# First four chunks of the second conditioning half: their own buffers, issued from ScalarE's queue

## The chip, the cores and the metric

The kernel runs on one core of a Trainium2 chip. Times are device microseconds (us) of one execution of the whole program; lower is better. The engines are TensorE (PE, matmuls; PEld, its weight loads), VectorE (DVE), ScalarE (ACT), GpSimd (POOL) and SyncE (SP). DMA transfers are issued from the queues of SP (q1 in the DMA lists), ACT (q10) and POOL (q0).

## What is computed

One block of a diffusion backbone: a conditioning vector c is turned by w_ada (2048 x 12288) into six modulation vectors; the first two are needed at once, the other four only later. The modulated latents (512 tokens) and context tokens (256) go through w_in, whose first 1024 columns (xa) feed a recurrent mixer.

```python
mod = silu_c @ w_ada[l] + b_ada[l]
mod_ctx = silu_cc @ w_ada[l] + b_ada[l]
sh1, sc1, g1, sh2, sc2, g2 = jnp.split(mod[:, None, :], N_ADA, axis=-1)
u_ctx = _modulate(_rms_norm(ctx, norm1_g[l]), sh1c, sc1c)
hc_f, hc_b = _bidir_rglru(u_ctx @ w_in[l][:, :D_LRU], *lru_p, h_zero, h_zero)
u = _modulate(_rms_norm(x, norm1_g[l]), sh1, sc1)
mix, _, _ = _mixer(u, rows, h0_f, h0_b, w_in[l], *lru_p, ...)
x = x + g1 * mix
x = x + g2 * _swiglu(_modulate(_rms_norm(x, norm2_g[l]), sh2, sc2), w_ffn_in[l], w_ffn_out[l])
```

## The kernel before, in words

Everything is written with explicit semaphores, one instruction stream for each engine, executed in the order of the code. All matmuls run in float32r as three products of a high and a low part: ACT copies a landed weight slice into its high part (`hi`, L826), DVE subtracts that from the slice to get the low part (`lo`, L2126), and PE multiplies (L1471 to L1473). This document calls the slices of w_in that go through the four-slot ring `w_raw` units; each is 128 x 1024 floats, 512 KB, and is loaded from SP's queue (L418).

**The first conditioning half** (the two modulation vectors that are needed at once) is read in 32 pieces into `ada_pq`, a ring of four slots of 8 KB per partition in the region `lru` (32 KB per partition). PE multiplies them (L1521) and counts them in `ada_used`. They come in eight ranges; after each, DVE and ACT scale and split two of the 16 feature slices of `u` and the context. Between the pieces PE already works on units 0 to 7 of xa.

**After the last range** SP has stored the transposed latents `x_raw` (4 MB, L450) and has issued units 8 and 9 right behind that store. Units 10 and later are each issued when the unit four places earlier has been used up (`unit_used`). The region `lru` now becomes `pad`, which takes the xa results, padded for a convolution: PE's banks are copied out by ACT (`xa_out`, L889) and by DVE (`xa_out`, L2248; it signals `ctx_free`). The first column half (heads 0 to 3) goes into the first 16 KB per partition, the second half (heads 4 to 7) into the last 16 KB. PE begins unit 8 only when the banks of column half 0 have been copied out by both engines. In DVE's stream that copy stands behind `lo` of unit 8 and `lo` of unit 9, and `lo` of unit 9 needs ACT's `hi` of unit 9, which needs unit 9 landed.

**The second conditioning half** is done without PE. It is read in chunks of 512 KB (128 rows of 1024 floats); DVE scales each chunk by one element of silu(c) and adds it to an accumulator (L2133 for the first of 16, L2136 for the others; it counts them in `ada2_used`), and PE sums each accumulator over the partitions at the end (`part_sums`, L1569). The first 32 chunks (0 to 31) are issued from POOL's queue (L755) into `ada2_pa`, four slots in the region `yx` that `x_raw` had; so POOL waits for the store of `x_raw` (`x_stored`) and for the last scaling. Chunk n from 4 on waits until chunk n-4 has been used. DVE takes them in fixed portions between the low parts of the units: behind `lo` of unit 10 chunks 0 to 4, behind `lo` of unit 11 chunks 5 to 9, and so on (`EARLY_CHUNKS`), chunks 28 to 31 behind `lo` of unit 16. PE runs units 8 to 15, then waits for chunk 31 (`part_sums`), then goes on with the windows of the recurrent mixer.

Of the kernel before, what the change touches and what calls it, by code (L numbers as in the profile page):

```python
# [21 lines left out]
F32 = mybir.dt.float32  # L22
# [6 lines left out]
D = 2048  # L29
T = 512  # L30
TC = 256
# [10 lines left out]
PADX = TC + 5  # L42
# [16 lines left out]
EARLY_CHUNKS = {8: 5, 9: 5, 10: 5, 11: 5, 12: 4, 13: 4, 14: 4, 15: 0}  # L59
N_EARLY = 32  # L60
N_MID = N_EARLY + 16
LANDED = (20 * 16, 20 * 16, 12 * 16, 12 * 16)


NPAIR = D_FF // P
# [39 lines left out]
class Chain:  # L105
# [5 lines left out]
    def link(self, ins):  # L111
        self.n += 1
        ins.then_inc(self.sem, 1)
        self.eng.wait_ge(self.sem, self.n + self.shift)
# [10 lines left out]
def build(nc, x, c, ctx_in, c_ctx, w_ada, b_ada, norm1_g, norm2_g, w_in, conv_w, conv_b, lru_wa, lru_ba,  # L125
          lru_wx, lru_bx, lru_lambda, w_lru_out, w_pool, pool_scale, w_fourier, b_gate, w_out,
          w_ffn_in, w_ffn_out, norm_f_g, consts, dft, out, x_fm):
    with ExitStack() as stack:

        kb = 1024  # L130
# [10 lines left out]
        def sb(name, region, shape, dt=F32, off=0):  # L141
            return nc.alloc_sbuf_tensor_at(name, [P, *shape], dt, offset=where[region] + off)
# [33 lines left out]
        pad = sb("pad", "lru", [HEADS, 1024])  # L176
# [72 lines left out]
        xcv_l = sb("xcv_l", "ada", [TCAT], F32R, 3 * kb)  # L249
        dft_t = sb("dft_t", "mix", [3, T], F32, 16 * kb)  # L250
        ada2_pa = sb("ada2_pa", "yx", [4, 1024])
        ada2_pc = sb("ada2_pc", "pf", [2, 1024])
        ada2_pw = sb("ada2_pw", "u_hi", [4, 1024], F32, 16 * kb)
        ada2_acc = sb("ada2_acc", "ada", [1024], F32, 8 * kb)
# [11 lines left out]
        cvec = misc("cvec", [KT, 2])  # L266
# [482 lines left out]
        @block.gpsimd  # L749
        def _(pool):  # L750
            def chunk(n, dst, slot=None):

                i, cc = n // 16, n % 16
                slot = n % 4 if slot is None else slot
                pool.dma_start(dst, ada_t[:, cc, 2 * D + 1024 * i:2 * D + 1024 * i + 1024]).then_inc(ada2_landed[slot], 16)  # L755

            pool.wait_ge(x_stored, 16)
            pool.wait_ge(u_aff, 2 * KT)
            for n in range(N_EARLY):
                if n >= 4:  # L760
                    pool.wait_ge(ada2_used, n - 3)
                chunk(n, ada2_pa[:, n % 4, :])
            for n in range(N_EARLY, N_MID):
                pool.wait_ge(ada2_used, n - 1)
                chunk(n, ada2_pc[:, n % 2, :], n % 2)
            for m in range(16):
                slot = (2, 3, 0, 1)[m % 4]
                if m == 2:
                    pool.wait_ge(lru_done, 8)
                pool.wait_ge(ada2_used, N_MID + m - (1 if m < 2 else 3))  # L770
                chunk(N_MID + m, ada2_pm[slot][:, :], slot)

            for p in range(PW - 1):
                pool.wait_ge(hid_done, p + 1)
                if p:
                    pool.wait_ge(gate_stored, 32 * p)
                for n, src in enumerate((silu_b, up_b)):
                    dst = mixed_fm[:, 2 * (p % 8) + n, :].rearrange("p (h n) -> p h n", n=TH)
                    if p < 8:
                        pool.dma_start(dst, src).then_inc(gate_stored, 16)  # L780
                    else:
                        pool.dma_start(dst, src, accum_op=ALU.add).then_inc(gate_stored, 16)

            pool.wait_ge(product_done, 7 * PW)
            for n in range(64, 128):
                pool.wait_ge(ada2_used, n - 3)
                chunk(n, ada2_pw[:, n % 4, :])

            def half_sums(p, b):

                landed = 16 * (p // 2) + 16
                pool.wait_ge(raw_landed[b]["S1"], landed - 16 * CW)
                pool.wait_ge(raw_landed[b]["A22"], landed)
                if p > PW:
                    pool.wait_ge(s1_added, 16 * (p - PW))
                pool.dma_start(wf[b]["S1"][:, :, :], wf[b]["A22"][:, :, :], accum_op=ALU.add).then_inc(s1_added, 16)
                pool.wait_ge(raw_landed[b]["S3"], landed)
                pool.wait_ge(raw_landed[b]["A11"], landed)
                if p > PW:
                    pool.wait_ge(s3_added, 16 * (p - PW))  # L800
                pool.dma_start(wf[b]["S3"][:, :, :], wf[b]["A11"][:, :, :], accum_op=ALU.add).then_inc(s3_added, 16)

            for p in range(PW, NALL):
                half_sums(p, p % 2)

            pool.wait_ge(x1_stored, 128)
            for u in range(3):
                pool.wait_ge(b_free[u], 1)
                pool.wait_ge(gate_stored, G_STORED + 16 * u)
                pool.dma_start(x1_fm[:, 2 * u:2 * u + 2, :], (stage1 if u == 1 else hidb)[:, :, :], accum_op=ALU.add).then_inc(gate_stored, 16)  # L810
            for a in range(ND):
                pool.wait_ge(s12_done, NALL + a + 1)
                pool.wait_ge(gate_stored, P_STORED + 32 * a)
                for n, src in enumerate((silu_b, up_b)):
                    dst = x1_fm[:, 2 * a + n, :].rearrange("p (h n) -> p h n", n=TH)
                    pool.dma_start(dst, src, accum_op=ALU.add).then_inc(gate_stored, 16)
# [3 lines left out]
        def _(act):  # L820
            chain = Chain(act, act_chain)

            def hi(base, per, i, u):

                landed(act, base, per, i, u)
                act.activation(w_hi[:, u % RING], w_raw[:, u % RING], ACT.Copy).then_inc(hi_done, 1)  # L826
# [60 lines left out]
            def xa_out(i, j):  # L887
                act.wait_ge(unit_used, 7 + j if i == 0 else 8 + 4 * j + 4)
                act.activation(pad[:, 4 * i + 2 * j:4 * i + 2 * j + 2, PADX:PADX + T], main[:, 2 * j:2 * j + 2, :],  # L889
                               ACT.Copy).then_inc(pair_free[j], 1)  # L890

            hi(0, 8, 0, 8)
            hi(0, 8, 0, 9)
            xa_out(0, 0)
            xa_out(0, 1)
            for u in range(8, 16):
                hi(0, 8, 0, u + 2)
                if u % 4 == 3:
                    xa_out(1, u // 4 - 2)
            sums_evac(2, 2, sums_row)  # L900

# [1216 lines left out]
        def _(dve):  # L2118
# [17 lines left out]
                    ins = dve.scalar_tensor_tensor(acc[:, :], src, k, acc[:, :], ALU.mult, ALU.add)  # L2136
                ins.then_inc(ada2_used, 1)

            def chunk_next(n, src, acc=None):
                dve.wait_ge(ada2_landed[n % 4], 16 * (n // 4 + 1))  # L2140
                chunk(src, n, cvec[:, n % 16, 0:1], acc)

            def mod2_out(a, b, n, bank):

# [94 lines left out]


            dve.wait_ge(ada_used, 32)
            dve.memset(pad[:, :, 0:2], 0.0)
            dve.memset(pad[:, :, 2 + TC:PADX], 0.0)
            link(dve.memset(pad[:, :, PADX + T:PADX + T + 1], 0.0))

            def xa_out(i, j):
                dve.wait_ge(unit_used, 7 + j if i == 0 else 8 + 4 * j + 4)
                dve.tensor_copy(pad[:, 4 * i + 2 * j:4 * i + 2 * j + 2, 2:2 + TC],  # L2248
                                aux[:, j, :].rearrange("p (n t) -> p n t", t=TC)).then_inc(ctx_free[j], 1)

            lo(0, 8, 0, 8)
            lo(0, 8, 0, 9)
# [1 line left out]
            xa_out(0, 1)  # L2254
            for u in range(8, 16):
                lo(0, 8, 0, u + 2)
                done = sum(EARLY_CHUNKS[v] for v in range(8, u))
                for n in range(done, done + EARLY_CHUNKS[u]):
                    chunk_next(n, ada2_pa[:, n % 4, :], ada2_acc1 if n // 16 == 1 else ada2_acc)
                if u % 4 == 3:  # L2260
                    xa_out(1, u // 4 - 2)

# [70 lines left out]
            def window(h, hh, p, base, per, i, u0, first=False, last=False):  # L2333
                for u in range(4):
                    lo(base, per, i, u0 + u + 2)
                    if u == 0:
                        gate_input_lo(h, p)
                    if u == 0 and not first:
                        mid(h - 1)
                        final(h - 1)  # L2340
                    if u == 1 and first:
                        mod2_out(0, 2, 1, main[:, 2, :])
                    if u == 2 and not first:
                        product(h - 1)
                    if u in (1, 2):
                        if first and u == 1:
                            dve.wait_ge(acc_used, 1)
                        dve.wait_ge(ada2_landed[u - 1], h * 16 + (4 * N_EARLY + 16))
                        chunk(ada2_pc[:, u - 1, :], h * 2 + (N_EARLY + u - 1),
                              cvec[:, ds(h * 2 + (u - 1), 1), 0:1].rearrange("p o n -> p (o n)"))  # L2350
                    if u == 3:
                        gate_input(h)
                        if not last:
                            conv(h + 1)
                        if not first:
                            product_lo(h - 1)
# [679 lines left out]
```

## Time and profile before

| | us |
|---|---|
| median of 3 runs | 2579.61 (2579.2 to 2579.81) |
| profiled execution, its own time | 2582.47 |
| its span, first to last instruction | 2580.7 |
| PE busy, share of the span | 99% |
| DVE / ACT / POOL busy | 77% / 47% / 8% |
| mean granted TensorE clock | 0.996 |

The page of the profile gives, for one execution, the busy share of each engine and the chain of work that ended last. The views used below are: the list of who waited for whom, the instructions in order of time (a line may merge several of the same kind; the idle time before it and what ended that idle time stand in brackets), the busy time of each engine in chosen stretches with the granted clock and the DMA share, and the DMA lists of a stretch (packets by queue; issues with the time from issue to landing). PE's busy share is high throughout, so only the places where it waits or where its clock is low can be won back.

### The profile page before, as it was taken

To read this page: it belongs to the slowest core of one execution; us is meant where nothing else is said; L and a number is where in the kernel's file an instruction comes from. 1 tells how busy PE (TensorE), PEld (TensorE's weight loads), DVE (VectorE), ACT (ScalarE), POOL (GpSimd) and SP (SyncE) were. 2 spreads that over 40 slices of the span, in tenths; PEclk is the share of its full clock that TensorE was granted. 3 is DMA by queue.
4 is the path that set the end of the run, shared out by engine and by line. 5 is a ranking of instruction groups with operands and counts; after the bars stand their busy time and mean duration, and the time that the engine had idled before them with its cause. 6 is when DMAs were issued, how large, how long until landed. Compare 5 with 4: busy or idle time off the path is not lost.

```text
span 2580.7 us, 39175 instructions
## 1 busy us (share of the span) xinstructions
PE 2552.7 (99%) x14527; PEld 2197.5 (85%) x14527; DVE 1983.7 (77%) x2223; ACT 1220.8 (47%) x1422; POOL 205.5 (8%) x277
## 2 busy tenths in 40 slices
PE   7999999999999999999999999999999999999998
PEld 6888888878888888888888888888888888888887
DVE  5567998778999999877967878777877767787443
ACT  4224887355555555422444444444444445455433
POOL 0010000000001111111000000000000000011000
PEclk8999999999999999999999999999999999999999
DMA  9985444755556666999668888888888864756644
GB/s 353 355 316 187 131 132 150 270 198 159 159 162 160 166 156 149 323 334 337 176 156 203 203 199 204 202 201 200 205 202 200 207 236 148 164 125 179 218 158 153
DMA packets 540412, 524.81 MB, mean 203 GB/s; under 512 B 16472, under 2 KB 491424, under 8 KB 535584
## 3 DMA queue, kind: packets, MB, share of 16 engines
q1 hardware_dynamic: 491296, 379.17, 47.8%
q0 software_dynamic: 44176, 126.90, 21.0%
q10 hardware_dynamic: 4848, 17.47, 1.7%
q8 instruction: 63, 1.03, 0.2%
q14 instruction: 29, 0.24, 0.0%
HBM read 427.00 MB, written 54.53 MB: 187 GB/s over the span
## 4 chain that ended last, share of the span: by engine, by line
PE 93%; DVE 3%; DMA 2%; ACT 1%; issue 1%; ACTq 0%; SPq 0%; DVEq 0%
PE main L1758 17%; PE aux L1758 17%; PE main L1765 9%; PE aux L1765 9%; PE main L1471 7%; PE main L1472 7%; PE main L1473 7%; PE aux L1999 3%; PE aux L1998 3%; PE aux L2000 3%; DMA ada_pa<-in_w_ada 1%; PE aux L1521 1%; PE main L1999 1%; PE main L2000 1%; PE main L1998 1%; PE aux L1471 1%
## 5 line engine op out<-in xcount | busy, mean ns | idle before, releaser
L2478 DVE TENSOR_TENSOR l_S<-f_S,h_S 128x1024 fp32r<-128x1024 f32 x288 | 344.9, 1219 | 15.3 <-ACT h_S L1056 15.3
L2478 DVE TENSOR_TENSOR l_A<-f_A,h_A 128x1024 fp32r<-128x1024 f32 x216 | 263.3, 1221 | 101.8 <-ACT h_A L1056 87.8
L1056 ACT ACTIVATE h_A<-f_A 128x1024 fp32r<-128x1024 f32 x216 | 226.6, 1051 | 221.2 <-PE aux L1765 111.6
L1056 ACT ACTIVATE h_S<-f_S 128x1024 fp32r<-128x1024 f32 x288 | 288.8, 1052 | 72.6 <-DVE f_S L2466 47.3
L1471 PE MATMUL main<-u_both,w_hi 128*128 128x512 f32 (+1 forms) x528 | 207.9, 394 | 0.3 <-DVE ctx_lo L2213 0.2
L1758 PE MATMUL main<-t_both,h_S 128*128 128x512 f32 x864 | 207.9, 389 | 0.2 <-DVE u_hi_spare L2531 0.2
L1758 PE MATMUL aux<-t_both,h_S 128*128 128x512 f32 x864 | 207.8, 389 | 0.0
L1472 PE MATMUL main<-u_both,w_hi 128*128 128x512 f32 (+1 forms) x528 | 203.7, 386 | 0.0
L1473 PE MATMUL main<-u_both,w_lo 128*128 128x512 f32 (+1 forms) x528 | 203.1, 385 | 0.0
L2126 DVE TENSOR_TENSOR w_lo<-w_raw,w_hi 128x1024 fp32r<-128x1024 f32 x120 | 146.0, 1221 | 64.7 <-ACT w_hi L826 64.5
L826 ACT ACTIVATE w_hi<-w_raw 128x1024 fp32r<-128x1024 f32 x120 | 125.8, 1053 | 147.6 <-DMA w_raw<-in_w_out 60.9
L1758 PEld LDWEIGHTS main<-t_both,h_S 128*128 128x128 f32 x864 | 161.9, 188 | 34.1 <-DVE u_hi_spare L2531 0.6
L1758 PEld LDWEIGHTS aux<-t_both,h_S 128*128 128x128 f32 x864 | 162.0, 188 | 33.5
L1758 PE MATMUL main<-u_both,h_A 128*128 128x512 f32 x576 | 144.2, 392 | 0.0
L1758 PE MATMUL aux<-u_both,h_A 128*128 128x512 f32 x576 | 144.1, 392 | 0.0
L2839 DVE TENSOR_TENSOR hb_l<-hb_f,hb_h 128x2048 fp32r<-128x2048 f32 x21 | 48.1, 2292 | 106.1 <-ACT hb_h L1331 106.1
L1471 PEld LDWEIGHTS main<-u_both,w_hi 128*128 128x128 f32 x528 | 99.8, 189 | 24.5 <-issue 5.0
L1758 PEld LDWEIGHTS aux<-u_both,h_A 128*128 128x128 f32 x576 | 103.8, 189 | 18.7
L1758 PEld LDWEIGHTS main<-u_both,h_A 128*128 128x128 f32 x576 | 103.6, 189 | 18.5
L1998 PE MATMUL aux<-hb_h,bw_h 128*128 128x512 f32 x304 | 118.9, 391 | 0.0
L2000 PE MATMUL aux<-hb_h,bw_l 128*128 128x512 f32 x304 | 118.3, 389 | 0.0
L1999 PE MATMUL aux<-hb_l,bw_h 128*128 128x512 f32 x304 | 118.3, 389 | 0.0
(363 smaller groups left out, 5637.1 us busy)
## 6 DMA issues: line engine op xcount, KB each, us to landing
f_A<-in_w_ffn_in SPq DMA_DIRECT2D x120, 512.0 KB, 5.3
f_S<-in_w_ffn_in SPq DMA_DIRECT2D x80, 512.0 KB, 5.7
f_S<-f_A POOLq DMA_DIRECT2D x80, 512.0 KB, 6.4
f_A<-in_w_in SPq DMA_DIRECT2D x72, 512.0 KB, 4.9
ada_pq<-in_w_ada SPq DMA_DIRECT2D x64, 512.0 KB, 8.5
ada_pw<-in_w_ada POOLq DMA_DIRECT2D x64, 512.0 KB, 6.2
bw_f<-in_w_ffn_out SPq DMA_DIRECT2D x56, 512.0 KB, 7.1
w_raw<-in_w_in SPq DMA_DIRECT2D x48, 512.0 KB, 4.7
```

What stands on the lines that cost most here:

```text
L826: act.activation(w_hi[:, u % RING], w_raw[:, u % RING], ACT.Copy).then_inc(hi_done, 1)
L1056: act.activation(wh[v][:, :, :], wf[b][v][:, :, :], ACT.Copy).then_inc(w_hi_done, 1)
L1471: pe.matmul(dst, wh, m_hi_ap, start=start, stop=False, skip_group_check=shared)
L1472: pe.matmul(dst, wh, m_lo_ap, start=False, stop=False, skip_group_check=shared)
L1473: return pe.matmul(dst, wl, m_hi_ap, start=False, stop=stop, skip_group_check=shared)
L1758: pe.matmul(dst, wh[v][:, k, :], moving[v](k)[0], start=start and k == 0, stop=False, skip_group_check=True)
L1765: ins = pe.matmul((aux, main)[b][:, bank, low * TH:low * TH + TH], wl[b][v][:, k, :], moving[v](k)[1], start=False, stop=k == HK - 1, skip ...
L1998: pe.matmul(dst, w_h, hb_h[b][:, cc, :], start=start and cc == 0, stop=False, skip_group_check=again)
L1999: pe.matmul(dst, w_h, hb_l[b][:, cc, :], start=False, stop=False, skip_group_check=again)
L2000: ins = pe.matmul(dst, w_l, hb_h[b][:, cc, :], start=False, stop=stop and cc == UC - 1, skip_group_check=again)
L2126: dve.tensor_tensor(w_lo[:, s], w_raw[:, s], w_hi[:, s].bitcast(F32), ALU.subtract).then_inc(lo_done, 1)
L2478: dve.tensor_tensor(wl[b][v][:, :, :], wf[b][v][:, :, :], wh[v][:, :, :].bitcast(F32), ALU.subtract).then_inc(w_lo_done, 1)
```

## The change

Chunks 0 to 3 get buffers of their own, `ada2_pl`, in the last 16 KB per partition of the region `lru` (slots 2 and 3 of the piece ring, later heads 4 to 7 of `pad`). ACT issues them, behind its splitting of the last range and ahead of `hi` of unit 8, once all 32 pieces have been used. POOL now issues chunks 4 to 7 without waiting for a chunk, at the place where it issued 0 to 3, and chunk n from 8 on waits for chunk n-4. DVE clears the edges of heads 4 to 7 of `pad` only behind chunk 3, and ACT waits for chunk 3 before it writes that half of `pad`. The counts of the landing semaphores are one transfer lower for each of POOL's slots, since four transfers now count on `ada_landed`.

```diff
-LANDED = (20 * 16, 20 * 16, 12 * 16, 12 * 16)
+LANDED = (19 * 16, 19 * 16, 11 * 16, 11 * 16)
+        ada2_pl = sb("ada2_pl", "lru", [4, 1024], F32, 16 * kb)
@@ gpsimd
-            for n in range(N_EARLY):
-                if n >= 4:
+            for n in range(4, N_EARLY):
+                if n >= 8:
                     pool.wait_ge(ada2_used, n - 3)
                 chunk(n, ada2_pa[:, n % 4, :])
@@ scalar
+            act.wait_ge(ada_used, 32)
+            for n in range(4):
+                act.dma_start(ada2_pl[:, n, :], ada_t[:, n, 2 * D:2 * D + 1024]).then_inc(ada_landed[n], 16)
             hi(0, 8, 0, 8)
             hi(0, 8, 0, 9)
...
                 if u % 4 == 3:
+                    act.wait_ge(ada2_used, 4)
                     xa_out(1, u // 4 - 2)
@@ vector
-            def chunk_next(n, src, acc=None):
-                dve.wait_ge(ada2_landed[n % 4], 16 * (n // 4 + 1))
-                chunk(src, n, cvec[:, n % 16, 0:1], acc)
+            def chunk_next(n, acc=None):
+                if n < 4:
+                    dve.wait_ge(ada_landed[n], 32 * 8 + 16)
+                else:
+                    dve.wait_ge(ada2_landed[n % 4], 16 * (n // 4))
+                chunk(ada2_pl[:, n, :] if n < 4 else ada2_pa[:, n % 4, :], n, cvec[:, n % 16, 0:1], acc)
...
-            dve.memset(pad[:, :, 0:2], 0.0)
-            dve.memset(pad[:, :, 2 + TC:PADX], 0.0)
-            link(dve.memset(pad[:, :, PADX + T:PADX + T + 1], 0.0))
+            def clear_edges(rows):
+                dve.memset(pad[:, rows, 0:2], 0.0)
+                dve.memset(pad[:, rows, 2 + TC:PADX], 0.0)
+                link(dve.memset(pad[:, rows, PADX + T:PADX + T + 1], 0.0))
+
+            clear_edges(slice(0, 4))
...
-                done = sum(EARLY_CHUNKS[v] for v in range(8, u))
-                for n in range(done, done + EARLY_CHUNKS[u]):
-                    chunk_next(n, ada2_pa[:, n % 4, :], ada2_acc1 if n // 16 == 1 else ada2_acc)
+                early_chunks(u)
+                if u == 8:
+                    dve.wait_ge(ada2_used, 4)
+                    clear_edges(slice(4, 8))
                 if u % 4 == 3:
                     xa_out(1, u // 4 - 2)
...
-                        dve.wait_ge(ada2_landed[u - 1], h * 16 + (4 * N_EARLY + 16))
+                        dve.wait_ge(ada2_landed[u - 1], h * 16 + 4 * N_EARLY)
```

## Rows read from the trace of the kernel before

**Rows 1.** Who waited for whom, PE, whole span: us in total, times, longest
```profile
PE main L1506 <- DMA x_tok<-in_x: 6.8, 1, 6.8
...
PE aux L1569 <- DVE ada_acc L2136: 2.0, 1, 2.0
PE main L1702 <- ACT bank_out L1007: 0.4, 1, 0.4
```
**Rows 2.** In order of time, PE: start us, us, engine, line, instruction
```profile
145.38 0.47 PE L1471 MATMUL main<-u_both,w_hi 128*128 128x512 f32 x1
...
212.83 0.28 PE L1473 MATMUL aux<-ctx_hi,w_lo 128*128 128x256 f32 x1
215.12 0.64 PE L1569 MATMUL aux<-ada_acc,pick 128*32 128x256 f32 x8 [2.01 <-DVE ada_acc L2136]
...
217.41 0.63 PE L1473 MATMUL main<-u_both,w_lo 128*128 128x512 f32 x1
217.84 0.63 PE L1471 MATMUL main<-u_both,w_hi 128*128 128x512 f32 x1
```
**Rows 3.** Stretches: busy us of PE, PEld, DVE, ACT, POOL; granted clock; DMA share; GB/s
```profile
139.00:142.00 3.00, 3.00 (x17) 2.55 (x17) 0.00 (x0) 1.06 (x1) 2.22 (x4) 1.00 0.61 164
142.00:151.60 9.60, 9.60 (x51) 8.12 (x50) 3.65 (x4) 3.97 (x4) 0.08 (x1) 1.00 0.87 317
...
215.00:220.00 5.00, 4.88 (x20) 3.60 (x21) 4.79 (x9) 1.33 (x2) 0.53 (x1) 0.66 0.93 339
```
**Rows 4.** In order of time, DVE: copies out for unit 8, chunks 0, 4, 7 and 8, 31
```profile
144.59 1.51 DVE L2248 COPY pad<-aux 128x512 f32<-128x512 f32 x2
...
152.86 0.75 DVE L2133 TENSOR_SCALAR ada_acc<-ada_pa,cvec 128x1024 f32<-128x1024 f32 x1
...
158.76 1.29 DVE L2136 SCALAR_TENSOR_TENSOR ada_acc<-ada_pa,cvec,ada_acc 128x1024 f32<-128x1024 f32 x1 [0.99 <-DMA ada_pa<-in_w_ada]
...
164.96 2.67 DVE L2136 SCALAR_TENSOR_TENSOR ada_acc<-ada_pa,cvec,ada_acc 128x1024 f32<-128x1024 f32 x2 [1.19 <-DMA ada_pa<-in_w_ada]
...
213.78 1.28 DVE L2136 SCALAR_TENSOR_TENSOR ada_acc<-ada_pa,cvec,ada_acc 128x1024 f32<-128x1024 f32 x1 [0.76 <-DMA ada_pa<-in_w_ada]
```
**Rows 5.** In order of time, ACT: end of the last range, units 8 to 10
```profile
137.46 0.49 ACT L877 ACTIVATE ctx_hi<-ctx_f,mod 128x256 fp32r<-128x256 f32 x1
140.78 1.06 ACT L826 ACTIVATE w_hi<-w_raw 128x1024 fp32r<-128x1024 f32 x1 [2.83 <-DMA w_raw<-in_w_in]
142.25 1.06 ACT L826 ACTIVATE w_hi<-w_raw 128x1024 fp32r<-128x1024 f32 x1 [0.40 <-DMA w_raw<-in_w_in]
...
150.63 1.06 ACT L826 ACTIVATE w_hi<-w_raw 128x1024 fp32r<-128x1024 f32 x1 [4.19 <-DMA w_raw<-in_w_in]
```
**Rows 6.** In order of time, POOL: issues of chunks 0 to 3, then chunk 8
```profile
139.78 2.31 POOL L755 DMA_DIRECT2D ada_pa<-in_w_ada  x4 [139.32 <-DMA x_feature_major<-x_raw]
...
160.36 0.53 POOL L755 DMA_DIRECT2D ada_pa<-in_w_ada  x1 [1.54 <-DVE ada_acc L2136]
```
**Rows 7.** In order of time, issues on SP's and ACT's queues: store, unit 12, a later store
```profile
122.71 1.41 SPq L450 DMA_DIRECT2D x_feature_major<-x_raw  x1
...
153.98 0.37 SPq L418 DMA_DIRECT2D w_raw<-in_w_in  x1
...
453.83 0.37 ACTq L998 DMA_DIRECT2D branches_feature_major<-bank_out  x1
```
**Rows 8.** DMA list, 140.0 to 141.6 us (queue: packets, MB, share of 16 engines)
```profile
q1 hardware_dynamic: 138, 0.13, 25.6%
```
**Rows 9.** The same, 148.8 to 149.6 us
```profile
q1 hardware_dynamic: 291, 0.29, 104.2%
```
**Rows 10.** The same, 142.0 to 144.4 us
```profile
q0 software_dynamic: 240, 0.91, 98.8%
```
**Rows 11.** The same, 144.8 to 147.6 us
```profile
q0 software_dynamic: 213, 0.81, 75.8%
q1 hardware_dynamic: 205, 0.21, 21.5%
```

More of the change, by code:

```diff
@@ L2249, in xa_out, with early_chunks @@
                                 aux[:, j, :].rearrange("p (n t) -> p n t", t=TC)).then_inc(ctx_free[j], 1)
+            def early_chunks(u):
+                done = sum(EARLY_CHUNKS[v] for v in range(8, u))
+                for n in range(done, done + EARLY_CHUNKS[u]):
+                    chunk_next(n, ada2_acc1 if n // 16 == 1 else ada2_acc)
             lo(0, 8, 0, 8)
```

## Prediction

> **What bounds the kernel now.** I read the list of PE's waits first, because PE is busy for 99% of the span: what can be won is PE's waiting and its low clock. Over the whole span there is little of either [rows 1]: waits for the first transfers and copies (the longest 6.8 us, all before 45 us and untouched by the change), one wait of 2.0 us for the accumulator of chunk 31, and nothing above 0.4 us behind it. The instructions in order of time show that wait: unit 15 ends at 212.95 (the last matmul issued at 212.83, one each 0.12 us), and PE goes on at 215.12 [rows 2]. The stretches give its second price, the clock: 0.66 in the five us behind the wait [rows 3]. There 512-column matmuls follow each other every 0.43 us (217.41, 217.84 [rows 2]), where at full clock it is 0.23 us, so the clock had gone from 2.4 to 1.2 GHz after PE had stood for 2 us. Nine matmuls at 0.43 in place of 0.23 cost 9 x 0.2 = 1.8 us; the granted clock gives 5 x 0.34 = 1.7; I take 1.7. So the place holds 2.1 + 1.7 = 3.8 us, 0.15% of the time, and no more can come out of the change. That is less than the 0.2% (5.2 us) that a measurement of this kernel can tell from no change.
>
> Then I read why chunk 31 is late. DVE begins chunk 0 at 152.86, behind `lo` of unit 10, which waits for that unit to land (ACT copies it as soon as it lands, at 150.63 [rows 5], and `lo` follows). Chunks 0 to 3 had landed by then, so what they wait for is unit 10, not their own transfers. From chunk 4 on DVE waits again and again for a chunk: four slots, each refilled some 6 us after its use (chunk 8 is issued at 160.36, 0.3 us after chunk 4 ends at 160.05, and used at 166.3 [rows 4, 6]).
>
> **Part 1: eight chunks ahead in place of four.** If DVE starts at 152.86 as now, chunks 4 to 7 are there and run back to back. Chunk 4 begins 0.99 us earlier (its idle time), chunk 7 another 1.19 earlier, 2.2 in all [rows 4]. Nothing more is gained later: chunk 8 still goes into a slot that chunk 4 frees, and so on in four chains, each of which keeps the lead that its first member had (0.99 for chunks 4, 5, 6; 2.2 for 7). Chunk 31 stands at the end of the best chain, but behind chunk 30, which is on a chain with 0.99; it was 0.76 late against its engine [rows 4]. So it ends 1.0 to 1.7 us earlier, at 213.4 to 214.1, still 0.4 to 1.1 us behind unit 15. The head start of four chunks is thus worth 1 to 1.7 us, plus the 1.7 of the clock if the wait left over is too short to drop it (0.4 us waits elsewhere did not).
>
> **Part 2: small edits.** The three clears of `pad` are split in two (each 0.07 us); the second set with its link adds about 0.3 us to DVE behind chunk 4. ACT's wait for `ada_used` costs nothing, since the range that it has just split needed all 32 pieces; its wait for chunk 3 stands ahead of the copy behind unit 11, four units of 8.5 us after 145.4 (eight units from 145.38 to 212.95 [rows 2]), so at 179, and chunk 3 is used by 158. POOL's issues 4 to 7 take the place of 0 to 3, at 139.78.
>
> **Part 3: four issues on ACT ahead of `hi` of unit 8.** ACT is free from 137.95 to 140.78 [rows 5]. The nearest row, an issue on this queue, is 0.37 us [rows 7]: four take 1.5 us and end at 139.5, hidden. The other end is 1.4 us, as the store on SP's backed-up queue [rows 7]: four end at 143.6, and `hi` of unit 9 would run at 144.6, 2.4 us late. I take 0.37, as ACT's queue is empty.
>
> **Part 4: 2.1 MB more in flight at 139 us.** This carries the sum. The DMA engines are nearly full from 142 to 151.6 (317 GB/s, share 0.87 [rows 3]). Unit 10 lands in that full stretch. 2.1 MB more take 2.1/0.37 = 5.7 us at the rate of rows 9 and 10 (0.29 MB in 0.8 us; 0.91 MB in 2.4 us), less what fits into the thin stretch 139 to 142 (164 GB/s of 370: 0.6 MB, 1.6 us). So units 10 and 11 land up to 4.1 us later, and chunk 0 starts at 155 to 157: 2 to 4 us late, more than the lead of part 1. DVE ends chunk 31 at 215.06 + (2 to 4) - (1 to 1.7), so at 215.4 to 218.1.
>
> Units 8 and 9 are nearer to PE. Unit 9 lands at 142.2, `hi` at 142.25, then `lo`, then DVE's copy, the first of the two from 144.59, which ends at 145.3; PE's unit 8 starts at 145.38, 0.16 us after unit 7's last matmul let it [rows 2, 4, 5]. So every us that unit 9 lands later is a us of PE. And unit 9 has a tail: at 140.0 to 141.6 only 138 of its 1 KB packets move [rows 8], 86 per us, where 16 engines move 364 [rows 9], 23 each. So some four engines (that they came late out of the 4 MB store of [rows 7] is my reading) still work through units 8 and 9: 2.6 us x 23 = 60 packets each from 139.2 to 141.8, of 64. ACT's chunks bring 32 packets of 4 KB to each engine. Where two queues have packets they alternate one to one: 213 against 205 [rows 11], and a 4 KB packet alone takes 2.4 x 16/240 = 0.16 us [rows 10], against 0.044 for 1 KB. So each packet of unit 9 on these engines waits 0.16 us more while ACT's last. When do they come? On an idle queue data moved 0.9 us after the issue (unit 12), after ACT's store at 453.83 it took 2.6 us [rows 7]; so from 138.9 to 140.6. Then 64 to 27 packets are left, and 27 to 32 of them alternate: 4.3 to 5.1 us. From 141 POOL's chunks are a third party: up to 23 rounds more, x 0.16 = 3.7 us, in all 8.8. Below zero is excluded: nothing here lets unit 9 land earlier. I take 6.0, the single alternation and a little of the second.
>
> The Trainium skill (DMA: Bandwidth & Descriptors, Issuing engines are not separate DMA queues) says that transfers started from several engines run on the same 16 DMA engines and interleave, and that this saves only issue time. The trace agrees (213 against 205 packets above), and it is this rule that speaks against the change. The page's section Queues, rings and completion order has each DMA engine go round the queues packet by packet; if it went through them first in, first out, unit 9 would not be touched, and the sum would be that of the second rival below.
>
> **The sum.** PE would start unit 8 at 151.4 instead of 145.4 and end unit 15 at 212.95 + 6.0 = 218.95. Chunk 31 ends by 218.1 and is no longer waited for, so the wait of 2.1 us goes and 6.0 come: 218.95 - 215.06 = +3.9. The clock drop behind the old wait (1.7) goes and one behind the new wait comes, at about the same price: 0. Behind 220 PE is bound by its own work to the end [rows 1], so the +3.9 stays. Against the profiled execution (2582.47, span 2580.7) that makes 2586.4; against the median, which is 2.9 lower, 2579.6 + 3.9 = 2583.5.
>
> **The rivals.** (a) Full alternation of three queues: unit 9 lands 7.3 to 9 us late, mostly 8.8, PE's unit 15 ends at 221.8: +6.7, 2586.3, slower by 0.26%. It decides from 7.3 us of delay of unit 9. For it: rows 6 and 8, POOL's chunks begin before the tail ends. Against it: in the trace of before the tail ran on beside POOL's first packets without visible delay. (b) ACT's data come only when units 8 and 9 are through (its queue was 2.6 us behind at 453.83); PE starts unit 8 on time, but unit 10 lands 2 to 4 us late, DVE starts late, and the wait at 213 stays or grows: +0.3 to +3.3, say +2: 2581.6. (c) It works as the diff says: units 8 to 10 land as now, the lead of 1 to 1.7 us and perhaps the clock: -1.0 to -3.3, 2577.5. Against it stand the full engines of rows 3.
>
> **How the numbers follow.** Forecast (unit 9 late by 4 to 7.3 us, +2 to +5.2): 0.38. (a) 0.26. (b) 0.20. (c) 0.14. The other 0.02 is a gain from elsewhere. Slower by over 0.2%: (a) and 0.02 of the forecast and of (b), 0.28. Faster by over 0.2%: 0.02, since the place holds 3.8 us. The rest, 0.70, is within 0.2%. The range leaves out the best part of (c) and the worst of (a): 2578.0 to 2587.2. The forecast's own range is 2581.6 to 2584.8.
>
> **What would show it.** Right: a wait of PE of 4 to 7 us at 145, ended by DVE's copy (L2248), a clock drop behind it, ACT's `hi` of unit 9 at 146 to 150 ended by a DMA, packets of q10 beside q1 at 139 to 142, and no wait of PE at L1569. (a) shows 7.3 us or more there, (b) no wait at 145 and a longer one at L1569, (c) a shorter one at L1569. The prediction is wrong if unit 9 still lands at 142 and unit 10 at 150.6.

## The result: 2583.97 us against 2580.0, slower by 0.16%

| | before | after |
|---|---|---|
| median, us | 2580.0 (2579.2 to 2582.62, 19 runs) | 2583.97 (2579.95 to 2587.91, 19 runs) |
| ratio of the medians | | 1.0016, 95% interval 1.0009 to 1.0022 |
| profiled execution, span | 2582.47, 2580.7 | 2580.99, 2579.2 |

The change costs 4 us, and single executions now spread over 8 us where those of before spread over 3.4. The two profiled executions stand the other way round: the one of before lies 2.5 us above its median, the one of after 3.0 below. Neither is typical, so the comparison of the two traces alone would say that the change gained 1.5 us. Most of what follows is about that.

**Profile after.** The waits of PE between 60 and 2500 us show what answers to rows 1. The wait for chunk 31 is gone, and in its place stands one before unit 8. The list puts it down to "issue", because it shows no releaser for it; DVE's copy in the rows below is what it ends with.

```profile
PE main L1476 <- issue: 1.6, 1, 1.6
```

The instructions of ACT in order of time (rows 5 of before) show the four issues, each 0.35 to 0.47 us and ended by 139.4, and units 8, 9 and 10:

```profile
137.59 0.35 ACTq L895 DMA_DIRECT2D ada_pl<-in_w_ada  x1
137.82 0.49 ACT L878 ACTIVATE ctx_hi<-ctx_f,mod 128x256 fp32r<-128x256 f32 x1
137.97 1.41 ACTq L895 DMA_DIRECT2D ada_pl<-in_w_ada  x3
140.93 1.06 ACT L827 ACTIVATE w_hi<-w_raw 128x1024 fp32r<-128x1024 f32 x1 [2.62 <-DMA w_raw<-in_w_in]
144.26 1.06 ACT L827 ACTIVATE w_hi<-w_raw 128x1024 fp32r<-128x1024 f32 x1 [2.27 <-DMA w_raw<-in_w_in]
...
154.15 1.06 ACT L827 ACTIVATE w_hi<-w_raw 128x1024 fp32r<-128x1024 f32 x1 [7.00 <-DMA w_raw<-in_w_in]
```

Unit 8 lands as before (140.93 against 140.78), unit 9 2.0 us later (144.26 against 142.25), unit 10 3.5 us later (154.15 against 150.63). DVE's rows (rows 4 of before) carry both on: the first of the two merged copies, the one that unit 8 needs, ends at 147.2 in place of 145.3 (0.68 us each), PE begins unit 8 at 147.28, and chunk 0 starts at 156.39 in place of 152.86. From there the head start works: chunks 0 to 8 run with only the clears and `lo` of unit 11 between them.

```profile
146.50 1.28 DVE L2259 COPY pad<-aux 128x512 f32<-128x512 f32 x2
155.24 1.23 DVE L2131 TENSOR_TENSOR w_lo<-w_raw,w_hi 128x1024 fp32r<-128x1024 f32 x1 [7.46 <-ACT w_hi L827]
156.39 0.75 DVE L2138 TENSOR_SCALAR ada_acc<-ada_pl,cvec 128x1024 f32<-128x1024 f32 x1
157.24 4.06 DVE L2141 SCALAR_TENSOR_TENSOR ada_acc<-ada_pl,cvec,ada_acc 128x1024 f32<-128x1024 f32 x3
161.40 1.28 DVE L2141 SCALAR_TENSOR_TENSOR ada_acc<-ada_pa,cvec,ada_acc 128x1024 f32<-128x1024 f32 x1
...
163.92 5.45 DVE L2141 SCALAR_TENSOR_TENSOR ada_acc<-ada_pa,cvec,ada_acc 128x1024 f32<-128x1024 f32 x4
...
213.16 1.29 DVE L2141 SCALAR_TENSOR_TENSOR ada_acc<-ada_pa,cvec,ada_acc 128x1024 f32<-128x1024 f32 x1 [0.67 <-DMA ada_pa<-in_w_ada]
```

The DMA list of this execution, 139.9 to 143.5 us (queue: packets, MB, share of 16 engines), shows who was there beside unit 9. ACT's queue (q10) carries the chunks, SP's (q1) ends its tail, and POOL's (q0), issued at 139.89, has moved nothing yet:

```profile
q10 hardware_dynamic: 338, 1.25, 87.0%
q1 hardware_dynamic: 191, 0.18, 15.1%
...
```

### The profile page after: what moved, and what is told of

The parts are those of the page before. It is cut to its first block, busy times and chain, and to the rows that moved or that the text cites. A ratio compares the mean times of both kernels' runs of the same rounds, so it can differ in the third digit from the quotient of the medians.

```text
span 2579.2 us, 39181 instructions
## 1 busy us (share of the span) xinstructions
PE 2552.5 (99%) x14527; PEld 2197.2 (85%) x14527; DVE 1983.7 (77%) x2226; ACT 1220.2 (47%) x1422; POOL 203.4 (8%) x273
## 3 DMA queue, kind: packets, MB, share of 16 engines
q8 instruction: 63, 1.03, 0.2%
## 4 chain that ended last, share of the span: by engine, by line
PE 95%; DVE 2%; DMA 1%; ACT 1%; issue 0%; ACTq 0%; SPq 0%; DVEq 0%
PE main L1763 17%; PE aux L1763 17%; PE main L1770 9%; PE aux L1770 9%; PE main L1476 8%; PE main L1477 8%; PE main L1478 8%; PE aux L2005 3%; PE aux L2003 3%; PE aux L2004 3%; PE aux L1526 1%; PE main L2005 1%; PE main L2004 1%; PE main L2003 1%; PE aux L1476 1%; PE aux L1477 1%
```

## The experiments

Theory T: the four transfers on ACT's queue share the DMA engines with the tail of units 8 and 9; unit 9 lands late by an amount that differs from execution to execution, and PE waits before unit 8. Beside it, unit 10 lands late and DVE starts the chunks late. Each kernel with an interval was compared with the kernel before, run beside it on the same chip.

| kernel | chip | median (lowest to highest), us | above before, us | ratio to before (95%) |
|---|---|---|---|---|
| changed kernel again | A | 2585.95 (2581.15 to 2590.11) | +6.0 | 1.0022 (1.0013 to 1.0031) |
| four unread transfers added to before | A | 2583.53 (2580.92 to 2588.98) | +3.6 | 1.0017 (1.0008 to 1.0026) |
| two unread transfers added to before | C | 2581.72 (2579.21 to 2585.94) | +1.8 | 1.0010 (1.0001 to 1.0019) |
| changed, ACT's issues behind unit 9 | A | 2581.55 (2579.13 to 2585.12) | +1.6 | 1.0007 (0.9998 to 1.0016) |
| changed, units 8 and 9 ahead of the store | A | 2582.23 (2580.48 to 2582.91) | +2.3 | 1.0007 (0.9998 to 1.0016) |
| changed, copy for unit 8 ahead of unit 9 | C | 2582.34 (2580.09 to 2584.13) | +2.4 | 1.0009 (1.0000 to 1.0018) |
| changed, POOL held back | B | 2583.51 (2579.76 to 2587.96) | +3.2 | 1.0014 (1.0005 to 1.0023) |
| changed, chunks ahead of unit 10 | B | 2583.46 (2579.72 to 2588.4) | +3.1 | 1.0014 (1.0005 to 1.0023) |
| before, chunks ahead of unit 10 | B | 2579.82 (2579.32 to 2581.78) | -0.5 | 0.9998 (0.9989 to 1.0007) |

All have 11 runs. The rows with the same letter ran beside each other on one chip; the kernel before had the medians 2579.95 (A), 2580.32 (B) and 2579.90 (C). An interval reaches 2.3 us to either side, so differences of 1 us between rows say little; the width of the spread says more.

### The kernel before, looked at again

> The kernel before once more, for a second profile, since the profiled execution of before (2582.47) lies 2.5 us above the median. T: PE waits 0 to 2 us for chunk 31, and the shorter the wait, the nearer the time to 2579. Rival R: the wait for chunk 31 is 2 us with its clock drop in every execution, and the time differs elsewhere.

2580.13 us, at the median. PE does not wait for chunk 31 at all. DVE's last chunks in order of time, and the stretch of PE behind them (columns as in rows 3):

```profile
207.73 2.67 DVE L2136 SCALAR_TENSOR_TENSOR ada_acc<-ada_pa,cvec,ada_acc 128x1024 f32<-128x1024 f32 x2 [0.34 <-DMA ada_pa<-in_w_ada]
210.32 1.22 DVE L2126 TENSOR_TENSOR w_lo<-w_raw,w_hi 128x1024 fp32r<-128x1024 f32 x1
```

```profile
210.00:215.00 5.00, 5.00 (x40) 4.21 (x39) 2.27 (x4) 1.27 (x3) 0.53 (x1) 1.00 0.68 212
215.00:220.00 5.00, 5.00 (x25) 4.10 (x23) 4.89 (x9) 0.98 (x2) 0.00 (x0) 1.00 0.51 155
```

Chunk 31 ends at 210.4, where it ended at 215.06 in rows 4, and the clock stays at 1.00, where rows 3 have 0.66. The wait of 2.1 us with 1.7 us of clock, on which my base rested, was there in one profiled execution and not in this one at the median. What PE does wait for here is unit 8, 0.4 us: unit 9 came at 142.79 in place of 142.25, so the kernel before already has almost no slack there.

### The changed kernel, three more profiles

> The changed kernel once more, for a second profile and its spread. Theory T (the four transfers on ACT's queue share the DMA engines with the tail of units 8 and 9, so unit 9 lands late by an amount that differs from execution to execution, and PE waits before unit 8): median 2582 to 2586, single times from 2580 to 2588, and the profile shows a wait of PE at 145 that is as long as its own time is above 2579. Rival R (the time differs for another reason, at the wait for chunk 31 or further on): the wait at 145 stays at the 1.6 us of the first profile whatever the time of the execution.

> The changed kernel, one more profile. T: if its time is above 2584, PE's wait before unit 8 is 4 us or more and there is no long wait for chunk 31; if it is below 2582, the wait before unit 8 is under 2 us.

> The same once more, with the same expectation: the time above 2579 is the wait before unit 8 and its clock drop, or a wait for chunk 31.

The median of the second set was 2585.95, 6.0 above before, and single times went up to 2590.11, above the 2588 expected. The profiles do not all fit the first expectation. The second (2582.01 us) is 3.0 above 2579 and yet has unit 9 on time (142.49), no wait before unit 8 and 1.4 us for chunk 31, so T missed there, and so did its rival, which wanted 1.6 us at unit 8. The third (2582.41, between the two bounds set for it) has unit 9 at 143.30, 0.3 us of wait before unit 8, and 2.5 us for chunk 31. The fourth, 2586.65 us, is what T expected: it shows what the long executions, which lift the median, pay for. Where the time goes in each of them can be read from PE's instructions (us; the time of the execution less the start of chunk 31's sums is in the last column):

| profile | its time | unit 8 begins | unit 15 ends | chunk 31's sums begin | time less that |
|---|---|---|---|---|---|
| before, first | 2582.47 | 145.38 | 212.95 | 215.12 | 2367.35 |
| before, second | 2580.13 | 145.96 | 213.53 | 213.62 | 2366.51 |
| changed, first | 2580.99 | 147.28 | 214.87 | 214.96 | 2366.03 |
| changed, second | 2582.01 | 146.73 | 214.26 | 215.86 | 2366.15 |
| changed, third | 2582.41 | 146.32 | 213.91 | 216.58 | 2365.83 |
| changed, fourth | 2586.65 | 150.25 | 220.40 | 220.49 | 2366.16 |

Behind chunk 31's sums all take the same time within 0.7 us, but for the first, which has the clock drop of rows 3 (1.7 us) in it. So what differs is decided by then: nothing further on is a rival. In the second profile PE came to unit 8 without a wait and still 1.35 us later than in the first of before. Most of that was there before the new transfers could act: ACT's first issue, which follows the last scaling, came 1.1 us later than in the first profile (138.73 against 137.59).

The next lines are from the fourth profile: PE's wait, ACT's instructions, and the stretches behind them.

```profile
PE main L1476 <- issue: 5.0, 1, 5.0
```

```profile
137.18 0.35 ACTq L895 DMA_DIRECT2D ada_pl<-in_w_ada  x1
...
140.99 1.06 ACT L827 ACTIVATE w_hi<-w_raw 128x1024 fp32r<-128x1024 f32 x1 [3.08 <-DMA w_raw<-in_w_in]
147.24 1.06 ACT L827 ACTIVATE w_hi<-w_raw 128x1024 fp32r<-128x1024 f32 x1 [5.19 <-DMA w_raw<-in_w_in]
```

```profile
144.00:150.00 6.00, 1.30 (x9) 1.02 (x7) 1.67 (x2) 2.76 (x3) 0.00 (x0) 0.90 1.03 398
150.00:153.00 3.00, 2.75 (x7) 2.20 (x8) 0.75 (x2) 0.12 (x1) 0.00 (x0) 0.50 0.95 347
153.00:156.00 3.00, 3.00 (x9) 2.39 (x8) 0.72 (x1) 1.57 (x2) 0.00 (x0) 0.55 0.22 77
156.00:159.00 3.00, 3.00 (x17) 2.52 (x17) 2.79 (x4) 0.55 (x1) 0.00 (x0) 1.00 0.00 0
```

Unit 9 lands at 147.2, PE stands for 5.0 us and then runs at 1.2 GHz (0.50) for 5.4 us, twelve to thirteen matmuls at 0.43 in place of 0.23: 2.5 us. Counted from 2579, about the lowest times of the kernel before, 5.0 + 2.5 = 7.5 us make 2586.5, against 2586.65 measured. The wait for chunk 31 is nil, since PE itself is late. The DMA list of 141.0 to 143.4 us shows who moved beside the tail of unit 9:

```profile
q10 hardware_dynamic: 250, 0.92, 95.2%
q1 hardware_dynamic: 52, 0.05, 7.4%
```

The 52 packets of SP's queue say little alone: the kernel before moves 55 in the same window, but all of them before 142, and unit 9 is in. Here the same tail is drawn out. From 142 to 144 us SP's queue moved no packet in the kernel before, and 2, 5, 22, 25 and 34 in the profiles that have `hi` of unit 9 at 142.49 (second), 143.30 (third), 144.26 (first), 145.15 (unread transfers, below) and 147.24 (fourth), while ACT's queue moved 203 to 225 in each of them. The more of unit 9 is left when ACT's packets run at full rate, the later it lands.

Put in order of ACT's first issue, the profiles of all kernels with four transfers there read as follows (issue, then `hi` of unit 9): 137.18 and 147.24 (fourth profile), 137.59 and 144.26 (first), 137.66 and 145.15 (unread transfers), 137.89 and 143.94 (copy first), 138.05 and 143.30 (third), 138.15 and 142.32 (POOL held back), 138.34 and 143.09 (chunks first), 138.73 and 142.49 (second). By and large, the earlier ACT issues, the later unit 9 lands; two pairs of neighbours stand the wrong way round, one of them with the kernel in which POOL was held back. ACT issues when PE has used the last piece, while the landing of unit 8 hardly moves (140.85 to 141.13 in these profiles), so the phase between the two looks like what makes one execution long and another short. That is an order seen in eight executions; the phase was not set by hand, and the cause of the spread is in so far not shown.

### The transfers without the head start

```diff
 # the changed kernel, but chunks 0 to 3 come from POOL as before
-            for n in range(4, N_EARLY):
-                if n >= 8:
+            for n in range(N_EARLY):
+                if n >= 4:
 # ACT's four transfers stay and nobody reads them; ACT and DVE wait for their landing before they use the place
-                    act.wait_ge(ada2_used, 4)
+                    for s in range(4):
+                        act.wait_ge(ada_landed[s], 32 * 8 + 16)
```

> The kernel before with the same four transfers added on ACT's queue, into the same buffers, read by nobody: chunks 0 to 3 still come from POOL, so there is no head start, only the 2.1 MB. T: PE waits at 145 as in the changed kernel, and chunk 0 starts 2 to 4 us late without a lead: 2583 to 2588, with single times spread over some 8 us. Rival E (what costs is the new order of chunks, waits and clears on DVE and ACT, not the transfers): 2580 to 2581, as before.

2583.53, 1.0017, with a spread of 8.1 us like that of the changed kernel: 2.1 MB on ACT's queue, read by nobody, bring a cost of 3.6 us and the spread. The changed kernel beside it had 6.0, the first set of the changed kernel 4.0, and the interval is 2.3 us to either side; so whether the other parts of the change cost anything is open, but they are not needed for the 4 us, and rival E is out. Its profile (2583.53, the median) has unit 9 at 145.15, chunk 0 at 157.31 (4.5 us later than in rows 4, a little more than the 2 to 4 expected), PE waiting 2.4 us and the clock at 0.87 from 150 to 160:

```profile
PE main L1477 <- issue: 2.4, 1, 2.4
```

```diff
-            for n in range(4):
+            for n in range(2):
                 act.dma_start(ada2_pl[:, n, :], ada_t[:, n, 2 * D:2 * D + 1024]).then_inc(ada_landed[n], 16)
```

> The kernel before with two of the four unread transfers on ACT's queue. T: half the packets to alternate with, so unit 9 is late by at most 2.6 us: 2580.5 to 2582.5, spread 3 to 5 us. Rival E (order, waits and clears, which are all kept here): as with four, 2583.5.

2581.72, 1.0010, with a spread of 6.7 us, wider than expected. The median lies between none and four, as the sizes do; the intervals overlap. Its profile (2580.68) has unit 9 at 143.72, 1.5 us later than in rows 5, and waits of 0.4 us before unit 8 and 0.7 us for chunk 31.

### Taking unit 9 out of the way

```diff
-            act.wait_ge(ada_used, 32)
-            for n in range(4):
-                act.dma_start(...)
             hi(0, 8, 0, 8)
             hi(0, 8, 0, 9)
+            act.wait_ge(ada_used, 32)
+            for n in range(4):
+                act.dma_start(...)
```

> ACT issues the four chunks behind hi of unit 9 in place of ahead of hi of unit 8, so that they start when unit 9 has landed. T: no wait of PE at 145 (under 0.3 us), unit 10 still lands late (152 to 156), chunk 0 starts at 154 to 158, and chunk 31 is again waited for: 2580 to 2583, with a spread much smaller than the 8 us of the changed kernel. Rival R: as the changed kernel, 2584 with its spread.

2581.55, 1.0007: 1.6 us above before, where the changed kernel beside it was 6.0 above, so 4.4 us come back. The profile (2580.61) has unit 9 at 142.93, unit 10 at 153.30, chunk 0 at 155.53, and PE waiting 0.3 us before unit 8 and 1.0 us for chunk 31. All is as expected, but for one run at 2585.12.

```diff
 # ACT (hi) and DVE (lo) alike
             hi(0, 8, 0, 8)
-            hi(0, 8, 0, 9)
             xa_out(0, 0)
+            hi(0, 8, 0, 9)
             xa_out(0, 1)
```

> The changed kernel, with the copy out for unit 8 (xa_out of column half 0, first bank pair) ahead of hi and lo of unit 9 on ACT and DVE in place of behind them; all transfers as they are. T (the loss is PE's wait before unit 8 through the late unit 9): no wait at 145 whatever unit 9 does, 2580 to 2581.5, and the spread shrinks from 8 us to 3. Rival R (the loss lies elsewhere, in unit 10, the chunks or further on): 2583 to 2586 with the spread of the changed kernel.

2582.34, spread 4.0 us: the highest time is 2584.13, where the changed kernel had 2587.91 and 2590.11. PE now needs unit 9 only when it has finished unit 8, 8.4 us later, so by an estimate from rows 2, 4 and 5 unit 9 may be some 9 us late without PE noticing. The median is 0.8 above what I expected. What is left looks like the other half of the theory, the late start of the chunks: its profile (2581.15) waits at the old place:

```profile
PE aux L1574 <- DVE ada_acc L2141: 1.9, 1, 1.9
```

```diff
-            sp.wait_ge(raw_out, 16)
-            sp.dma_start(x_fm, x_raw[:, :, :]).then_inc(x_stored, 16)
-            for u in range(8, 16):
+            for u in range(8, 10):
+                xa_unit(u)
+            sp.wait_ge(raw_out, 16)
+            sp.dma_start(x_fm, x_raw[:, :, :]).then_inc(x_stored, 16)
+            for u in range(10, 16):
                 xa_unit(u)
```

> The changed kernel with units 8 and 9 issued on SP ahead of the 4 MB store in place of behind it. T: units 8 and 9 land before 132, no wait of PE at 145, chunk 0 still starts late (unit 10 lands at 152 to 155): 2579 to 2582, small spread. Rival R: 2584 with the spread of the changed kernel.

2582.23, and the narrowest spread of the changed kernels, 2.4 us. Units 8 and 9 were in by about 133 (132 expected; the last of their packets move between 132 and 133). But PE does wait before unit 8, 1.6 us, and not for unit 9: ACT is held by its own issues.

```profile
137.84 0.35 ACTq L897 DMA_DIRECT2D ada_pl<-in_w_ada  x1
138.07 0.49 ACT L880 ACTIVATE ctx_hi<-ctx_f,mod 128x256 fp32r<-128x256 f32 x1
138.23 4.72 ACTq L897 DMA_DIRECT2D ada_pl<-in_w_ada  x3
143.00 2.01 ACT L829 ACTIVATE w_hi<-w_raw 128x1024 fp32r<-128x1024 f32 x2 [4.44 <-issue]
```

Three issues take 4.72 us in place of 1.41. They end at 142.95, just when the 4 MB store lands (issued at 125.42, 17.6 us to landing). The expectation was wrong on that; it is the upper end of part 3 of the prediction, met in another kernel.

### The third queue, and the order of the chunks

```diff
             pool.wait_ge(u_aff, 2 * KT)
+            pool.wait_ge(lo_done, 10)
             for n in range(4, N_EARLY):
```

> The changed kernel, with POOL's chunks 4 to 7 held back until lo of unit 9 is done. Theory T2 (ACT's queue alone delays unit 9; in the first profile POOL's data begin only at 143.6): the median stays within 1.5 us of the changed kernel and the spread too. Rival A (three queues alternate on unit 9, and POOL's is half of the delay): the wait at 145 shrinks by half or more, 2579 to 2582.

2583.51, spread 8.2 us: the long executions come without POOL's chunks too, so its transfers have no visible part in the median or the spread, and half of the delay, as rival A has it, does not fit. Its profile (2579.83) is one of the short ones: unit 9 at 142.32, unit 10 already at 148.90, chunk 0 at 151.13, and no wait of PE at either place. So chunk 31 had room here, and the median was still 3.2 us above before.

```diff
-                lo(0, 8, 0, u + 2)
-                early_chunks(u)
                 if u == 8:
+                    early_chunks(u)
+                    lo(0, 8, 0, u + 2)
                     dve.wait_ge(ada2_used, 4)
                     clear_edges(slice(4, 8))
+                else:
+                    lo(0, 8, 0, u + 2)
+                    early_chunks(u)
```

> The changed kernel with the same change in DVE's order. T: chunk 0 starts at 147 to 149 in place of 156.4 and PE does not wait for chunk 31, but the four transfers on ACT's queue still let unit 9 land late: 2578 to 2584 with the spread of the changed kernel, and slower than the kernel before with this order by 2 to 6 us. Rival H: no different from the changed kernel, 2584 to 2586.

> The kernel before, with one change in DVE's order: chunks 0 to 4 ahead of lo of unit 10 in place of behind it; no transfer moves. T (what holds chunk 0 back is unit 10, not its own transfer): chunk 0 starts at 146 to 147 in place of 152.9, chunk 4 at 153 to 154 in place of 158.8, chunk 31 ends 3 to 5 us earlier and PE does not wait for it, and the spread stays that of before: 2576 to 2578. Rival H (chunk 31 is bound by the four slots and their refills alone, whatever the start): as before, 2579 to 2580.

The same order was tried in the kernel before. There chunk 0 starts at 147.06 and chunk 4 at 154.01, as expected, and chunk 31 ends at 208.6, but the time is 2579.82, not 2576 to 2578: a miss. The profile of before at 2580.13 says why: at the median there was no wait left to win. In the changed kernel chunk 0 starts at 147.12, chunk 31 is off the path too (ended at 209.6), and the time stays at 2583.46 with the full spread. The two differ by 3.6 us with chunk 31 out of play in the profiles of both. Both profiles are of short executions (2580.16 and 2581.19), and in neither does PE wait before unit 8; that the 3.6 us are the price of the transfers at unit 9 follows from the other experiments and from the spread, 8.7 us against 2.5, and was not seen in a long execution of this kernel. No version beat the kernel before by more than its interval.

## Why the prediction was right, and where it was not

The direction, the cause and the range were right: the transfers delay unit 9, PE waits for it, and unit 10 and the chunks are late. That the sum gave +3.9 us and the medians differ by 4.0 is luck. The sum was 6.0 of delay less 2.1 of a wait that goes, with nothing for the clock. The delay was put too high, the wait was mostly not there to be saved, and the clock cost 2.5 us in the long execution; the errors cancel. The same kernel measured a second time was 6.0 above. Of the signs that I set for being right (a wait of 4 to 7 us at 145, `hi` of unit 9 at 146 to 150, a clock drop, no wait for chunk 31) the first profile shows only the last, and only the fourth shows all.

**The base.** "Chunk 31 is no longer waited for, so the wait of 2.1 us goes" failed against the median. The wait was real in the profiled execution of before, 2582.47 us, and absent in the second profile, 2580.13. I had seen that the profiled execution was 2.9 us above the median and carried this over as a constant; it was largely that wait. At the median, as far as that one profile speaks for it, next to nothing of the 3.8 us could be won, whatever the change did.

**Part 4, unit 9.** The mechanism is shown: the transfers alone bring the cost and the spread, issuing them behind unit 9 takes 4.4 us of 6.0 away, letting PE start without unit 9 cuts off the longest times, and the longest profiled execution has the wait. The size is the term that I had wrong in kind. I took 6.0 us late; the four profiles of the changed kernel have 2.0, 0.2, 1.1 and 5.0 us (144.26, 142.49, 143.30, 147.24 against 142.25). The second profile of before had 142.79, so half a microsecond of this is there without the change. It is a spread, not a number, and my 4.3 to 5.1 for one alternation is the upper part of it; the 6.0 that I took lies above all four. ACT's first data moved 1.4 us after its first issue (139.0 against 137.59), inside my 0.9 to 2.6 us; read again, those two bounds are 1.0 and 2.9 us (first packets at 155.0 and 456.7). A delay of 5.0 without the credit for the base, with 2.5 of clock, gives the 7.5 us of the fourth profile; the median lies halfway. The longest single time, 2590.11, was not profiled, so how late unit 9 can come is open.

**Part 4, unit 10 and DVE.** Unit 10 landed at 154.2 to 154.5 (forecast: up to 4.1 later than 150.6), chunk 0 began at 156.4 to 156.7 (forecast 155 to 157), chunk 31 ended at 214.5, 215.8, 216.5 and 216.1 (forecast 215.4 to 218.1). This step held but for the 214.5, and it costs where unit 9 is on time: 1.4 and 2.5 us of wait in the second and third profile.

**Part 1.** The lead of 1 to 1.7 us was not measured by itself: the start moved with it. From the start of chunk 0 to the end of chunk 31 the two profiles of before take 62.2 and 58.0 us, the four of the changed kernel 58.1, 59.1, 60.0 and 59.6. I had reckoned with this as a constant; it varies by more than the lead. What the runs bound is the lead's worth at the median, which is nil within the interval, as the chunks-first order of the kernel before shows.

**Part 3** held (1.8 us for four issues against 1.5), with its other end seen when units 8 and 9 stand ahead of the store.

**The clock.** I priced any 2 us wait of PE at 1.7 us of clock. In the third profile PE waited 2.5 us and the clock stayed at 1.00 behind it (213 to 222), and so it did behind 1.6 us in the first; behind 2.0 in rows 3 and behind 2.4 with the unread transfers (0.57 from 150 to 153) it fell, and behind 5.0 it was low for 5.4 us. The price of a short wait is not fixed.

**The rule of the Trainium skill** (DMA: Bandwidth & Descriptors, Issuing engines are not separate DMA queues) held: a second issuing queue brought no engines of its own, only one more party on the same ones. From 144 to 150 us their share was 1.01 in the first profile of before and 1.03 in the first of the changed kernel, full both times (362 and 401 GB/s, the latter with more 4 KB packets among them). First in, first out, the alternative that I named beside the other section, does not fit: it would have left unit 9 on time, and ACT's 250 packets moved while it was outstanding.

**The rivals.** (a) is not needed: the long executions come with POOL held back too, and in the first profile POOL's data began only when unit 9 was all but in (143.8 against 144.26). In the fourth they began at 143.8 while unit 9 landed at 147.2, so in the longest executions POOL may have had a part. (b) has the outcome of the second and third profile, but not by its reason: ACT's data began 1.0 us after the issue, before units 8 and 9 were in. (c) appears in no profile of the changed kernel.

## What to carry to other kernels

Before costing a wait of 2 us in a 2.6 ms kernel, profile the kernel twice: where the profiled execution lies off the median, the wait may be what makes it so. A prefetch that is moved earlier competes with whatever is landing then; look first for the transfer with no slack (here unit 9, 0.16 us) and for its tail, and put the new issues behind it. If a load must share the engines, reorder the consumer so that the copy which frees the matmul does not stand behind the load that comes next. And where a sum agrees with the result to 0.1 us, check its terms one by one before believing it.

## What was not expected of the hardware

- The queue that came second moved nothing for some 4 us. POOL's transfers, issued at 139.89, moved their first data at 143.8 with ACT's queue busy (no packet of q0 from 139.9 to 143.5); in the kernel before, issued at 139.78, they began at 141.2 and filled the engines from 142 (rows 10). With ACT's issues behind unit 9 it was the other way round: POOL's data began at 142.0, and ACT's, issued at 142.93, at 146.9.
- Four issues on ACT's queue took 1.8 us, but 5.1 us in the profile in which the 4 MB store on SP's queue was still on its way until 143.0.
- A shift of ACT's first issue by 1.5 us (137.2 to 138.7) went with 5 us of difference in the landing of another queue's transfer.
- The granted clock stayed at 1.00 behind waits of 1.4, 1.6, 1.9 and 2.5 us and fell behind waits of 2.0, 2.4 and 5.0 us.
